# Attention loop of a two-block layer stack: query blocks from last to first, head outputs taken first, transposes ahead of the memory unit

## The chip, the cores and the metric

One core of one Trainium2 chip runs the whole program. The metric is the device time of one execution in microseconds. The times of before are those of 3 runs.

## What is computed

Two layers of a first block (gated short convolution, retention, squared-ReLU MLP) on 512 tokens of width 1024, and then one layer of a second block. The change lies in the second block's mixer, and in the rotary tables of the first. Cut to what matters:

```python
def nsa_mixer(q, k_c_raw, v_c_raw, k_s, v_s, k_w, v_w, gate_logits, ...):
    ...
    s_c = einsum(qb, k_cmp) * scale            # 31 compressed keys
    p_c = masked_softmax(s_c, cmp_end <= t)
    ...                                        # 8 key blocks, 16 to be chosen: all are
    p_s = masked_softmax(s_s, kpos <= t)
    p_w = masked_softmax(s_w, (kp <= t) & (kp > t - WINDOW))
    ...
    o = g0 * o_c + g1 * o_s + g2 * o_w

def gmlp_mixer(z, ...):                        # v normalised, mixed over 128 tokens
    return u * mixed
def conformer_conv_mixer(z, ...):              # 31 taps, layer norm, silu
    ...
def memory_cross_attention(x, mem, ...):       # k, v from 256 memory tokens
    ...
def rotary(t, positions):                      # first block: cos and sin of the angles
    ...
```

With 512 tokens the selected and the window attention are both plain causal attention, for 8 heads of width 64 in 2 key groups.

## The kernel before, in words

Everything is kept transposed: features on partitions, 512 tokens in the free dimension. Each matrix product is cut in units of 128 output columns. For a unit SyncE loads 512 KB of weights into one of two `raw` buffers, ScalarE rounds them to fp32r (`wh`, L451 in straight code, L504 in the layer loop), GpSimd subtracts to get the rest (`wl`, L422, two halves), and TensorE does 24 matmuls, high by high, high by low and low by high, in one of two PSUM banks. A load waits for the `wl` of two units before, ScalarE's split for the matmuls of four units before.

**The start.** ScalarE splits x and the first four weight units, then waits for the rotary angles from VectorE (L484), takes sine and cosine (L485, L486) and enters its loop over the two layers (L493). There `ahead(VV, f)` waits for unit f's matmuls and splits unit f + 4, and after f = 3 the square root of the mean square is taken (L491). The eight units VV are of another form (L1708): four token blocks in four banks, and the second four of them use `aux`; its bank 3 also holds the mean square, so that TensorE waits for the root before it starts on that bank.

**The attention loop.** After the input products of the second block come 16 steps. `ITS` lists pairs (c, rp), query block c of 128 tokens and head pair rp, and each pair has two steps b = 0, 1 (selected and window attention), each with 4 heads. Step k has scores against (c + 1) * 128 keys. A list `TURNS` gives the blocks of 128 probabilities to be transposed: for b = 0 the compressed block (31 keys) and c + 1 others, for b = 1 c + 1. In each iteration k of the written-out loops:

- TensorE (L1969): the ones-matmul of a norm at steps 3, 7, 8 and 10 (`mixer_norms`, L1884), the scores of step k + 1 (L1897, after the exps of step k), one unit of the memory's keys or values (`mem_unit`, L1780, 24 matmuls of 256 columns), then `values(k - 1)`: it waits for the weighed probabilities of step k - 1 and, for b = 0, for `o_taken`; it transposes block by block (L1917, L1919), and after each transpose multiplies the block before with the values (L1933), all into one bank, `unit_ps[1]`.
- ScalarE (L719): exps of heads 0 and 1 of step k + 1 (L669), copy of the memory unit (L714), split of the next weights (L451), then by turns the copy of a transposed block of step k - 1 (`take_turn`, L678) and exps of heads 2 and 3.
- VectorE (L1444): `shift(k + 1)` adds the mask on the diagonal block and takes the negative maximum (L1326, L1328), `weigh(k)` multiplies the four heads by gate over sum (L1336, L1342), for b = 1 `take_out(it - 1)` copies the finished outputs of the pair before (L1181), three taps of the 31-tap convolution (L1215; 62 in all, 36 of them before the loop), and pieces of the three norms (L1390, L1401, L1411, L1421, L1430). What is left of the taps is done at once before the sum of step 6.

Ahead of the loop stand the mixing over tokens (`mix_mm`, L1959, after the last query unit), its use on VectorE (L1382), and the compressed scores (L1903), which use the same two banks. Behind it, the squares of the attention outputs are summed and averaged (L1997), and the eight parts are normalised (L1471, L1478) for the first output unit (L1794), in the order of `PART_ORDER`.

## Time and profile before

| | us |
|---|---|
| median of 3 runs | 2635.04 |
| lowest, highest | 2633.44, 2638.72 |
| the profiled execution, own time | 2637.93 |
| its span | 2636.1 |
| TensorE busy (with overlaps of pipelined matmuls taken out) | 2542.3 (96%) |
| VectorE busy | 1237.7 (47%) |
| ScalarE busy | 907.2 (34%) |
| GpSimd busy | 1252.6 (48%) |
| granted TensorE clock, mean | 0.979 |

A granted clock of 1.00 is 2.4 GHz, 0.50 is 1.2 GHz. Spans of back-to-back matmuls overlap in the trace: the distance of their starts is what one costs.

### The profile page before, as it was taken

To read this page: it belongs to the slowest core of one execution; us is meant where nothing else is said; L and a number is where in the kernel's file an instruction comes from. 1 tells how busy PE (TensorE), PEld (TensorE's weight loads), DVE (VectorE), ACT (ScalarE), POOL (GpSimd) and SP (SyncE) were. 2 spreads that over 40 slices of the span, in tenths; PEclk is the share of its full clock that TensorE was granted. 3 is DMA by queue.
4 is the path that set the end of the run, shared out by engine and by line. 5 is a ranking of instruction groups with operands and counts; after the bars stand their busy time and mean duration, and the time that the engine had idled before them with its cause. 6 is when DMAs were issued, how large, how long until landed. Compare 5 with 4: busy or idle time off the path is not lost.

```text
span 2636.1 us, 34492 instructions
## 1 busy us (share of the span) xinstructions
PE 2542.3 (96%) x11696; PEld 2056.3 (78%) x11696; DVE 1237.7 (47%) x1471; ACT 907.2 (34%) x1281; POOL 1252.6 (48%) x879
## 2 busy tenths in 40 slices
PE   8999999999999999999999999999777799999998
PEld 6887788888888888877888888888644487888887
DVE  5434612452322543451245332268776654788373
ACT  4223433332222422343333222243345433444233
POOL 4554355555555555534555554555322142555454
PEclk8999999999999999999999999999888899999999
DMA  4333133333333333323333333363111031333332
GB/s 146 100 95 88 56 96 96 97 95 98 99 96 98 93 101 96 92 59 88 96 96 96 96 96 97 102 152 89 57 48 41 25 95 48 96 96 96 98 99 74
DMA packets 448120, 236.23 MB, mean 90 GB/s; under 512 B 16144, under 2 KB 442256, under 8 KB 447888
## 3 DMA queue, kind: packets, MB, share of 16 engines
q1 hardware_dynamic: 446896, 232.38, 30.6%
q10 hardware_dynamic: 1120, 2.51, 0.3%
q8 instruction: 61, 1.00, 0.2%
q14 instruction: 43, 0.35, 0.0%
HBM read 232.76 MB, written 2.10 MB: 89 GB/s over the span
## 4 chain that ended last, share of the span: by engine, by line
PE 89%; DVE 6%; issue 2%; ACT 1%; POOL 1%; DMA 0%; DVEq 0%; ACTq 0%; POOLq 0%
PE unit_ps L1673 58%; PE unit_ps L1794 16%; PE unit_ps L1780 7%; PE aux L1708 2%; PE o_banks L1738 1%; DVE a_f L1342 1%; DVE row L1328 1%; PE unit_ps L1933 1%; DVE c_f L1215 1%; PE aux L1726 1%; POOL wl L422 1%; PE o_banks L1919 1%; PE aux L2009 1%; DVE aux L1326 0%; PE unit_ps L1708 0%
## 5 line engine op out<-in xcount | busy, mean ns | idle before, releaser
L422 POOL TENSOR_TENSOR wl<-raw,wh 128x512 fp32r<-128x512 f32 x862 | 1246.1, 1466 | 1363.4 <-ACT wh L504 853.3
L504 ACT ACTIVATE wh<-raw 128x1024 fp32r<-128x1024 f32 x304 | 322.3, 1061 | 1028.1 <-PE unit_ps L1673 975.3
L1673 PE MATMUL unit_ps<-ah,wh 128*128 128x512 f32 x1280 | 503.5, 393 | 3.6 <-DVE tmp L1072 3.6
L1673 PE MATMUL unit_ps<-al,wh 128*128 128x512 f32 x1280 | 499.5, 390 | 0.0
L1673 PE MATMUL unit_ps<-ah,wl 128*128 128x512 f32 x1280 | 499.5, 390 | 0.0
L1673 PE MATMUL unit_ps<-bh,wh 128*128 128x512 f32 x768 | 299.7, 390 | 0.0
L1673 PE MATMUL unit_ps<-bl,wh 128*128 128x512 f32 x768 | 298.8, 389 | 0.0
L1673 PE MATMUL unit_ps<-bh,wl 128*128 128x512 f32 x768 | 298.8, 389 | 0.0
L1673 PEld LDWEIGHTS unit_ps<-ah,wh 128*128 128x128 f32 x1280 | 241.2, 188 | 55.9 <-DVE tmp L1072 4.4
L1673 PEld LDWEIGHTS unit_ps<-al,wh 128*128 128x128 f32 x1280 | 240.9, 188 | 51.4 <-issue 1.9
L1673 PEld LDWEIGHTS unit_ps<-ah,wl 128*128 128x128 f32 x1280 | 241.1, 188 | 50.5
L451 ACT ACTIVATE wh<-raw 128x1024 fp32r<-128x1024 f32 x111 | 117.6, 1060 | 205.3 <-PE unit_ps L1794 111.9
L1673 PEld LDWEIGHTS unit_ps<-bh,wh 128*128 128x128 f32 x768 | 144.2, 188 | 30.8 <-issue 1.0
L1673 PEld LDWEIGHTS unit_ps<-bl,wh 128*128 128x128 f32 x768 | 144.2, 188 | 30.3 <-issue 0.5
L1673 PEld LDWEIGHTS unit_ps<-bh,wl 128*128 128x128 f32 x768 | 144.2, 188 | 29.9
L1146 DVE TENSOR_TENSOR x<-unit_ps,x 128x512 f32 x48 | 33.2, 691 | 213.5 <-PE unit_ps L1673 213.5
L1794 PE MATMUL unit_ps<-ch,wh 128*128 128x512 f32 x320 | 124.5, 389 | 0.0
L1794 PE MATMUL unit_ps<-cl,wh 128*128 128x512 f32 x320 | 124.5, 389 | 0.0
L1794 PE MATMUL unit_ps<-ch,wl 128*128 128x512 f32 x320 | 124.5, 389 | 0.0
L1136 DVE TENSOR_TENSOR tmp<-unit_ps,rstd 128x512 f32<-128x512 f32 x64 | 44.2, 691 | 135.7 <-PE unit_ps L1673 134.9
L1569 DVE SCALAR_TENSOR_TENSOR d<-tmp,vectors,d 128x511 f32<-128x511 f32 x88 | 106.1, 1205 | 1.5
L1673 PE MATMUL unit_ps<-ch,wh 128*128 128x512 f32 x256 | 99.6, 389 | 0.0
(349 smaller groups left out, 3876.6 us busy)
## 6 DMA issues: line engine op xcount, KB each, us to landing
raw<-w_in_dram SPq DMA_DIRECT2D x147, 512.0 KB, 4.0
raw<-w_up_dram SPq DMA_DIRECT2D x64, 512.0 KB, 4.0
raw<-w_down_dram SPq DMA_DIRECT2D x64, 512.0 KB, 4.0
raw<-up_dram SPq DMA_DIRECT2D x44, 512.0 KB, 3.8
raw<-w_conv_out_dram SPq DMA_DIRECT2D x16, 512.0 KB, 4.0
raw<-w_ret_out_dram SPq DMA_DIRECT2D x16, 512.0 KB, 3.9
raw<-w_o_dram SPq DMA_DIRECT2D x16, 512.0 KB, 4.0
raw<-down_dram SPq DMA_DIRECT2D x16, 512.0 KB, 3.8
```

Of the source, the lines that this page charges most:

```text
L422: last = pool.tensor_tensor(wl[j][:, half], raw[j % 2][:, half], wh[j][:, half].bitcast(F32), ALU.subtract)
L451: act.activation(wh[j][:], raw[j % 2][:], ACT.Copy).then_inc(w_hi, 1)
L504: act.activation(wh[j][:], raw[j % 2][:], ACT.Copy).then_inc(w_hi, 1)
L1136: dve.tensor_tensor(tmp[0][:], unit_ps[j % 2][:], rstd[:], ALU.mult).then_inc(evac, 1)
L1146: dve.tensor_tensor(blk(x, f), unit_ps[j % 2][:], blk(x, f), ALU.add).then_inc(evac, 1)
L1215: did(dve.scalar_tensor_tensor(out=cv_a[i], in0=src, scalar=w, in1=cv_a[i], op0=ALU.mult, op1=ALU.add))
L1328: did(dve.tensor_reduce(row[:, 4 * b, heads], aux[:, heads, 0:nk], AX, ALU.max, negate=True), shift_att)
L1569: did(dve.scalar_tensor_tensor(out=into, in0=tmp[n % 2][:, 0:T - s_], scalar=ffn_taps[:, w_, b:b + 1], in1=into, op0=ALU.mult, op1=ALU.add ...
L1673: last = pe.matmul(unit_ps[j % 2][:], w[j][:, k], v[:, k * T:(k + 1) * T], start=(k == 0 and n == 0), stop=(k == KB - 1 and n == 2))
L1708: last = pe.matmul(v_ps[group][c], v[:, col:col + P], two_k(w[j])[:, k], start=(k0 + k == 0 and w is wh and v is ah), stop=(k0 + k == KB - ...
L1780: last = pe.matmul(dst, w[u % 4][:, k], v[:, k * n:(k + 1) * n], start=(k == 0 and q == 0), stop=(k == n_k - 1 and q == 2))
L1794: last = pe.matmul(unit_ps[u % 2][:], w[u % 4][:, k], v[:, k * T:(k + 1) * T], start=(at == 0 and q == 0), stop=(at == n_k - 1 and q == 2))
```

## The change

It does seven things. The query blocks go from c = 3 to c = 0 (`ITS`). VectorE does `take_out` before `shift` and `weigh`. TensorE transposes the first two blocks of step k - 1 before the memory unit, and the others two ahead of the values; ScalarE copies them before exps 0 and 1 of step k + 1. The convolution's sums and norm move from step 7 to step 9, with three taps in every step until then. The mixing over tokens goes ahead of the last query unit, and its VectorE part too, in the place of two taps. The reciprocal for the norm of x goes to step 7, its products from steps 13 and 14 to steps 14 and 15. At the start, sine and cosine go behind the square root of the first layer, and ScalarE's loop over the two layers is written out.

```diff
-ITS = [(c, rp) for c in range(NC) for rp in range(REP // 2)]
+ITS = [(c, rp) for c in reversed(range(NC)) for rp in range(REP // 2)]
...
-GM_STEP, CV_STEP = 3, 7
+GM_STEP, CV_STEP, TAPS_IN_STEP = 3, 9, 3
...
# ScalarE
-            act.wait_ge(ang_done, 1)
-            act.activation(sin[:], sin[:], ACT.Sin).then_inc(trig_done, 1)
-            act.activation(cos[:], cos[:], ACT.Sin).then_inc(trig_done, 1)
-            act.wait_ge(ones_set, 1)
...
-            with act.Fori(0, LAYERS) as l:
+            for l in range(LAYERS):
...
                     if f == 3:
                         sqrt_ms(l * 2 + 1)
+                        if l == 0:
+                            act.wait_ge(ang_done, 1)
+                            act.activation(sin[:], sin[:], ACT.Sin).then_inc(trig_done, 1)
+                            act.activation(cos[:], cos[:], ACT.Sin).then_inc(trig_done, 1)
...
-                if more:
-                    exp_head(k + 1, 0)
-                    exp_head(k + 1, 1)
+                turns = turns_of(k - 1)
+                for n in range(2):
+                    if n < len(turns):
+                        take_turn(*turns[n])
+                    if more:
+                        exp_head(k + 1, n)
                 mem_copy(k)
                 ahead2(MK + k)
-                turns = turns_of(k - 1)
-                for n in range(max(len(turns), 2)):
-                    if n < len(turns):
-                        take_turn(*turns[n])
-                    if more and n < 2:
-                        exp_head(k + 1, 2 + n)
+                for turn in turns[2:3]:
+                    take_turn(*turn)
+                if more:
+                    exp_head(k + 1, 2)
+                for turn in turns[3:4]:
+                    take_turn(*turn)
+                if more:
+                    exp_head(k + 1, 3)
+                for turn in turns[4:]:
+                    take_turn(*turn)
...
# VectorE
             z_query(2)
-            some_taps(2)
+            dve.wait_ge(mix_mm, 2)
+            for i in range(2):
+                ...
+                mult(y_gm[i], gm_u[i], tmp[1][:], mixed)
             z_query(3)
...
-                elif k == CV_STEP + 5:
+                elif k == CV_STEP - 2:
                     go()
                     did(dve.reciprocal(rstd_x, rstd_x))
-                if k in (CV_STEP + 6, CV_STEP + 7):
+                if k in (CV_STEP + 5, CV_STEP + 6):
                     for n in range(4):
-                        first_norm(4 * (k - CV_STEP - 6) + n)
+                        first_norm(4 * (k - CV_STEP - 5) + n)
...
                 mixer_norms_first(k)
+                if b == 1 and it:
+                    take_out(it - 1)
                 if k + 1 < N_STEPS:
                     shift(k + 1, 0)
                     shift(k + 1, 1)
                 if k == 0:
                     compressed_weights()
                 weigh(k)
-                if b == 1 and it:
-                    take_out(it - 1)
-                some_taps(3)
+                some_taps(TAPS_IN_STEP)
                 mixer_norms_last(k)
...
# TensorE
-            for f in range(Z_KW, Z_Q + 4):
+            for f in range(Z_KW, Z_Q + 3):
                 z(f)
...
+            def first_turns(k):
+                it, b, c, rp = STEPS2[k]
+                if b == 0:
+                    pe.wait_ge(pc_ready, 1)
+                pe.wait_ge(p_ready, k + 1)
+                for j in turns_of(k)[:2]:
+                    turn_block(j)
+
             def values(k):
                 it, b, c, rp = STEPS2[k]
-                mine = [j for j, turn in enumerate(TURNS) if turn[0] == k]
-                pe.wait_ge(p_ready, k + 1)
-                if b == 0:
-                    pe.wait_ge(pc_ready, 1)
-                    if it:
-                        pe.wait_ge(o_taken, it)
+                if b == 0 and it:
+                    pe.wait_ge(o_taken, it)
+                mine = turns_of(k)
                 for j in mine:
-                    turn_block(j)
-                    if j > mine[0]:
-                        block_values(j - 1)
-                block_values(mine[-1])
+                    block_values(j)
+                    if j + 2 <= mine[-1]:
+                        turn_block(j + 2)
...
                         if i and c == NC - 1:
                             last.then_inc(mix_mm, 1)
+            z(Z_Q + 3)
...
-                mem_unit(k)
                 if k == 0:
                     pe.wait_ge(shift_cmp, 1)
                 else:
+                    first_turns(k - 1)
+                mem_unit(k)
+                if k:
                     values(k - 1)
+            first_turns(N_STEPS - 1)
             values(N_STEPS - 1)
```

## Rows read from the trace of the kernel before

**Rows 1.** Stretches: length; busy PE, PEld, DVE, ACT, POOL; clock; DMA share, GB/s.
```profile
100.00:1750.00 1650.00, 1646.25 (x7185) 1346.58 (x7184) 614.64 (x751) 510.63 (x615) 837.30 (x581) 1.00 0.33 95
1866.30:2096.40 230.10, 167.06 (x1028) 113.26 (x1027) 160.41 (x245) 105.48 (x239) 45.35 (x34) 0.82 0.14 42
```

**Rows 2.** Waits of TensorE, 1866 to 2097 us: total, times, longest.
```profile
PE o_banks L1917 <- DVE d L1181: 22.2, 7, 5.6
PE unit_ps L1933 <- ACT a_f L678: 10.4, 14, 1.6
```

**Rows 3.** Waits of VectorE, the same stretch.
```profile
DVE aux L1326 <- PE aux L1897: 35.5, 8, 9.8
...
DVE d L1401 <- PE unit_ps L1884: 2.2, 1, 2.2
```

**Rows 4.** ScalarE in order of time, at the start: start, length, what, wait before it.
```profile
21.07 1.28 ACT L485 ACT_TABLE_LOAD   x1
34.50 0.63 ACT L485 ACTIVATE sin_t<-sin_t 128x512 f32<-128x512 f32 x1 [12.15 <-DVEq L895]
...
36.96 2.00 ACT L504 ACTIVATE wh<-raw 128x1024 fp32r<-128x1024 f32 x2
...
49.07 0.69 ACT L491 ACTIVATE rstd<-aux,eps 128x512 f32<-128x512 f32 x1
```

**Rows 5.** TensorE in order of time, at the start.
```profile
38.07 1.22 PE L1708 MATMUL aux<-wh,ah 128*128 128x512 f32 x2 [5.20 <-ACT wh L504]
...
49.81 1.22 PE L1708 MATMUL aux<-wh,ah 128*128 128x512 f32 x2 [3.16 <-ACT rstd L491]
...
69.05 0.39 PE L1673 MATMUL unit_ps<-ah,wh 128*128 128x512 f32 x1
```

**Rows 6.** SyncE's queue: the issue of the load of unit 4.
```profile
21.70 0.37 SPq L321 DMA_DIRECT2D raw<-w_in_dram  x1
```

**Rows 7.** The same load, then that of unit 6: KB, us to landing.
```profile
raw<-w_in_dram SPq DMA_DIRECT2D x1, 512.0 KB, 5.3
...
raw<-w_in_dram SPq DMA_DIRECT2D x1, 512.0 KB, 3.6
```

**Rows 8.** GpSimd in order of time, low parts of units 4 and 5.
```profile
38.10 4.97 POOL L422 TENSOR_TENSOR wl<-raw,wh 128x512 fp32r<-128x512 f32 x4 [13.02 <-ACT wh L504]
```

**Rows 9.** TensorE in order of time, ahead of the loop.
```profile
1866.24 1.97 PE L1959 MATMUL o_banks<-d,c_f 128*64 128x128 f32 x32
...
1872.02 6.88 PE L1903 MATMUL o_banks<-k_cmp,c_f 64*128 64x31 f32 x64 [3.17 <-DVE d L1177]
```

**Rows 10.** VectorE in order of time, in the loop and behind it.
```profile
1891.38 1.25 DVE L1342 TENSOR_SCALAR a_f<-a_f,row 128x128 f32<-128x128 f32 x4
...
1895.56 0.42 DVE L1328 TENSOR_REDUCE row<-aux 128x2 f32<-128x256 f32 x1
...
1897.49 3.20 DVE L1342 TENSOR_SCALAR a_f<-a_f,row 128x128 f32<-128x128 f32 x4
...
2010.09 1.23 DVE L1328 TENSOR_REDUCE row<-aux 128x2 f32<-128x1024 f32 x1
...
2067.54 2.05 DVE L1342 TENSOR_SCALAR a_f<-a_f,row 128x512 f32<-128x512 f32 x4
...
2081.66 0.43 DVE L1181 COPY d<-unit_ps 128x256 f32<-128x256 f32 x1 [11.54 <-PE unit_ps L1933]
```

**Rows 11.** TensorE in order of time, in the loop: at half clock, then at full.
```profile
2022.12 1.12 PE L1919 MATMUL o_banks<-ident,a_f 128*128 128x128 f32 x4
...
2025.07 2.34 PE L1897 MATMUL aux<-c_f 64*128 64x512 f32 x8
...
2030.32 0.82 PE L1919 MATMUL o_banks<-ident,a_f 128*128 128x128 f32 x6
...
2072.81 0.65 PE L1933 MATMUL unit_ps<-a_f,c_f 128*64 128x256 f32 x4
2073.40 0.66 PE L1919 MATMUL o_banks<-ident,a_f 128*128 128x128 f32 x4
```

More of the change, by code:

```diff
@@ L1314, in _ @@
             z_query(2)
-            some_taps(2)
+            dve.wait_ge(mix_mm, 2)
+            for i in range(2):
+                go()
+                biased = tmp[1][:].rearrange("p (c t) -> p c t", c=NC)
+                did(dve.tensor_tensor(biased, o_ps[i].rearrange("p (c t) -> p c t", c=NC), gm_bias[:, i].unsqueeze(1).broadcast_to([P, NC, P]), ALU.add))
+                mult(y_gm[i], gm_u[i], tmp[1][:], mixed)
             z_query(3)
@@ L1376, in compressed_weights @@
                 mult(p_cmp, p_cmp, by_head.unsqueeze(3).broadcast_to([P, 2, NC * REP, N_CMP]), pc_ready)
-            dve.wait_ge(mix_mm, 2)
-            for i in range(2):
-                go()
-                biased = tmp[1][:].rearrange("p (c t) -> p c t", c=NC)
-                did(dve.tensor_tensor(biased, o_ps[i].rearrange("p (c t) -> p c t", c=NC), gm_bias[:, i].unsqueeze(1).broadcast_to([P, NC, P]), ALU.add))
-                mult(y_gm[i], gm_u[i], tmp[1][:], mixed)
             shift(0, 0)
@@ L1935, in block_values, with turns_of @@
                         last.then_inc(o_att, 1)
+            def turns_of(k):
+                return [j for j, turn in enumerate(TURNS) if turn[0] == k]
+            def first_turns(k):
[5 more added lines that the diff above has]
+                    turn_block(j)
             def values(k):
                 it, b, c, rp = STEPS2[k]
-                mine = [j for j, turn in enumerate(TURNS) if turn[0] == k]
-                pe.wait_ge(p_ready, k + 1)
-                if b == 0:
-                    pe.wait_ge(pc_ready, 1)
-                    if it:
-                        pe.wait_ge(o_taken, it)
+                if b == 0 and it:
+                    pe.wait_ge(o_taken, it)
+                mine = turns_of(k)
                 for j in mine:
-                    turn_block(j)
-                    if j > mine[0]:
-                        block_values(j - 1)
-                block_values(mine[-1])
+                    block_values(j)
+                    if j + 2 <= mine[-1]:
+                        turn_block(j + 2)
             pe.wait_ge(gm_ready, 1)
```

## The prediction

> **What bounds the kernel now.** I read the stages first. From 100 to 1750 us TensorE is busy for 1646 of 1650 us at full clock [rows 1]: nothing on ScalarE, VectorE or GpSimd can help or hurt there as long as it stays hidden. The first 100 us and the attention stretch (1866 to 2096 us, TensorE busy 167 of 230 us, granted clock 0.82) are where an order of instructions can matter. Then I read the waits of that stretch. TensorE waits 22.2 us before the first transpose of a query block (L1917), seven times for the VectorE copy at L1181, which is `take_out` [rows 2]. VectorE waits 35.5 us for score matmuls [rows 3] and 11.5 us for the last values [rows 10]. So the two wait for each other in turn; the loop is a chain, and neither is full. The reader is to see that `take_out(it-1)` needs values finished long ago, but stands behind `shift(k+1)` and `weigh(k)`.
>
> **Part 1, the sine and cosine.** ScalarE loads the Sin table at 21.07, stands until 34.50 for VectorE's angles, reloads, and only at 36.96 splits weight unit 4 [rows 4]. Behind it hang the unit's low part, the next two loads, the square root at 49.07, and TensorE: it starts unit 4 at 38.07, stops before bank 3 and goes on at 49.81 with 78 matmuls left until 69.05 [rows 5]. After the change the split waits for the data alone. The load was issued at 21.70 [rows 6] and took 5.3 us [rows 7]: 27.0. Then split 1.05 (28.1), low part 2.5 (30.6; four halves took 4.97 [rows 8]), low part of unit 5 another 2.5 (33.1), load of unit 7 3.6 [rows 7] (36.7), its split 1.05, table load 1.28, root 0.69: 39.8 against 49.8. **Minus 10.0 us.** TensorE is free for unit 4 at 32.9 (38.07 less its wait of 5.20 [rows 5]); 18 matmuls of 0.229 (1646 us for 7185 [rows 1]) bring it to bank 3 at 37.0, so it stands 2.8 us, where before it stood twice. Before, the last 78 matmuls took 19.2 us instead of 17.8, the first of them at half clock; if the clock stays at 2.4 GHz another 1.4 us go. Bounds: minus 7 (loads later behind the decay table) to minus 11.5. Sin and cos themselves (1.2 us and a table load) now follow the root, beside matmuls, and end near 42; VectorE, in its 3.35 us reciprocal, asks for them later. If that cover went they would cost 2.5 us. Unrolling the layer loop on ScalarE touches only the stretch where TensorE is full: 0, bounds plus or minus 1 (one more or less table load of 1.28 a layer).
>
> **Part 2, the memory mixing ahead of the last query unit.** Now z(Z_Q+3) ends, mixing takes 1.97, and TensorE waits 3.17 us for VectorE before the compressed scores at 1872.02, which then take 6.88 us with 64 matmuls [rows 9], at 1.2 GHz. After: query unit 3 ends 2 us later (1868.3), one evacuation of about 0.7, scores of step 0 for four key blocks 2.0 (2.3 in rows 11, partly at half clock): 1871, with no wait. At full clock the 64 take about half, ending at 1875; at half clock at 1878. I take 1875. But steps 0 and 1 are now blocks of 512 keys: VectorE's reduction is 1.23 instead of 0.42 [rows 10], two per shift, so shift(1) costs 1.6 more, weigh(0) 0.8 more (2.05 against 1.25, rows 10). `weigh(0)` ended at 1892.63. **Minus 1.5**, bounds plus 1.5 to minus 3. The two taps left out here come back in the loop.
>
> **Part 3, the loop.** From the end of weigh(0), 1892.63, to the end of the last copy before the drain, 2070.1 (2081.66 less the wait of 11.54 [rows 10]), VectorE spends 177.5 us; 35.5 + 2.2 are waits [rows 3], so 139.8 is work. After: two of the long shifts and one weigh moved out in front, minus 3.3 and 0.8; two taps more, plus 1.6. Then collisions: a weigh of four 128x128 took 3.20 us while GpSimd subtracted a weight unit and 1.25 us while it didn't [rows 10], 1.95 per unit. Of the 16 units I count six whose subtraction now falls in VectorE's waits or reciprocals; with the waits gone about three more collide, plus 5.5. Work 142.8.
> Waits: `take_out` first costs VectorE 0.5 us in another place and nothing new, since TensorE finished those values one iteration before. It frees TensorE's 22.2 us. Transposes of two blocks ahead of the memory unit hide ScalarE's copies behind 24 matmuls (the waits for them at L1933 were 10.4 us [rows 2]). TensorE's own period for four key blocks is per pair of steps 2 x 2.0 scores, 2 x 3.0 memory units (from the scores' end to 2030.32), 9 blocks of 1.2 (transposes and values, 0.66 and 0.65 long, each beginning a little before the other ends) = 20.8 [rows 11]; VectorE's is about 21. For one key block 11.5 against 14 with reciprocals. So VectorE bounds, and its waits go except in the convolution's norm chain: there TensorE's mean waits for VectorE's sum and VectorE for the mean. These now lie in steps 9 to 12. From each step's durations I get 2 us at step 9 (the mean), 5.5 at step 10 (the variance behind a memory unit at half clock) and 3.5 in steps 11 to 13: 11 in all, bounds 4 and 24 (the waits at the chain now). Sum 153.8 against 177.5: **minus 23.7**. The five taps in a lump before step 7 go into steps 7 and 8, the same work. The reciprocal of rstd_x at step 7 and first_norm one step later are moved, at 0.
>
> **Part 4, the drain.** VectorE is through at 2070.1, and the next copy waits 11.54 us until 2081.66 [rows 10], because the last two steps have five and four blocks to transpose and multiply. With blocks from last to first it is two and one, and VectorE still has four norm products to do: 0.5 remains. **Minus 11.0**, bounds minus 8 and 11.5. The 14.3 us from there to TensorE's restart don't change.
>
> **ScalarE and the queues.** exp_head now stands behind take_turn, so behind `weigh(k-1)`; that one ended before the shift whose result exp_head needs, so 0. If weigh ran late each exp would slip with it. Weight loads are issued per unit as before, one in 6 us or more.
>
> **Sum.** 10.0 + 1.5 + 23.7 + 11.0 = 46.2 off the profiled execution's 2637.9: 2591.7. The median of the runs is 2.9 lower than that execution, so I give 2589.
>
> **A rule against it.** In the rows a collision costs 1.95 us per unit, and the rest of the two subtractions runs beside VectorE. The Trainium skill, "SBUF — State Buffer", section "Who interferes with whom", says the pair of ports that VectorE and GpSimd share is an exclusive lock and the loser fully blocks for the whole instruction. By that rule every unit could cost its whole subtraction.
>
> **Rivals.**
> A. *Collisions fill the gain.* If all 16 units blocked VectorE for their 2.5 us, that is 40 us against the about 17 lost now, plus 23 instead of plus 5.5: 2606. For it: VectorE is now dense. Against: rows 10 show 1.95, and reciprocals and shifts run free. 0.12.
> B. *The norm chain stays single file.* All 24 us of waits stay in the short last steps, where TensorE has least to do: 2602. For it: the longest wait, 9.8 [rows 3], was there. 0.14.
> C. *The start doesn't shrink*, since loads of units 6 and 7 come later: 2599. 0.05.
> D. *The other side: TensorE stays at 1.2 GHz through the loop.* At full clock it has 48 blocks x 1.2 + 16 x 3.0 + 24 of scores = 130 us; at half a transpose group lasts 1.12 instead of 0.66 [rows 11], 1.7 times as long: 221 us against today's 199 from 1882.9 to 2081.66, plus 22, less 4 for the earlier start and 10 of part 1: 2643. It decides once TensorE spends some four fifths of the loop at half clock. The clock is 0.82 today, and the half-clock pieces follow the waits for take_out, which go. 0.04.
> E. *The order was not the limit*: something I don't see holds the pair, and only part 1 offsets new frictions: within 0.2% of before. 0.02.
> The forecast itself, 2577 to 2598: 0.57; still lower, 0.06.
>
> **The numbers.** Low 2574 is all parts at their good bounds nearly (11.5 + 3 + 35 + 11.5); high 2612 takes in A, B and C and A with B in part. A measurement of this kernel tells 0.2% (5 us) from no change. Faster 0.94, same 0.02, slower 0.04.
>
> **What would show it.** In the changed profile: the root before unit 4's bank 3 near 40 and the first L1673 matmul near 58; no wait of L1917 for L1181; VectorE's score waits about 11 us, at steps 9 to 12; the last take_out within 2 us of the norm products; output units going on near 2050 of the new span, where they did at 2096. Wrong if TensorE's clock in the loop is under 0.6, or if VectorE's taps and weighs average more than a third above today's.

## The result, and the profile after

| | before | after |
|---|---|---|
| median, us (4 runs each) | 2634.24 | 2590.52 |
| lowest, highest | 2632.62, 2638.72 | 2589.98, 2591.71 |
| the profiled execution, own time | 2637.93 | 2590.40 |
| its span | 2636.1 | 2588.6 |
| TensorE busy | 2542.3 (96%) | 2524.0 (98%) |
| granted TensorE clock, mean | 0.979 | 0.986 |

The ratio of the runs is 0.9835 (95% interval 0.9822 to 0.9847): the changed kernel is 43.7 us faster by the medians. The profiled executions are 47.5 us apart, because that of before lies 3.7 us above its own median. Sums over stages below are of those two executions.

The changed kernel by stretches: length; busy PE, PEld, DVE, ACT, POOL; clock; DMA share, GB/s. The rows are the step ahead of the loop, the loop to the last copy, the drain to TensorE's restart, and all that is behind it.

```profile
1859.60:1881.80 22.20, 14.67 (x112) 8.82 (x112) 18.87 (x27) 11.22 (x23) 5.17 (x4) 0.80 0.17 48
1881.80:2034.10 152.30, 129.25 (x872) 90.50 (x872) 129.72 (x203) 86.70 (x205) 40.12 (x30) 0.91 0.17 49
2034.10:2048.90 14.80, 6.80 (x11) 2.99 (x11) 12.39 (x15) 7.21 (x11) 0.00 (x0) 0.59 0.12 33
2048.90:2588.60 539.70, 527.08 (x2361) 431.54 (x2361) 322.53 (x317) 211.14 (x295) 260.82 (x184) 0.99 0.29 86
```

The reader is to compare the second row with the kernel before over the same work:

```profile
1892.60:2070.10 177.50, 130.11 (x760) 85.76 (x760) 129.39 (x201) 84.51 (x196) 37.90 (x29) 0.83 0.14 42
```

VectorE is busy for about the same 129 us (its gaps between instructions not counted) in 152 us instead of 177. The work did not shrink; the standing did. Where the 47.5 us between the spans came from:

| stretch | before | after | difference | predicted |
|---|---|---|---|---|
| start, to the first 512-column unit | 69.05 | 61.59 | −7.5 | −10.0 |
| from there to the end of `weigh(0)` | 1823.6 | 1820.2 | −3.4 | −1.5 |
| loop, to the end of VectorE's last work before the last copy | 177.5 | 152.2 | −25.3 | −23.7 |
| that end to the start of the last copy | 11.5 | 0.1 | −11.4 | −11.0 |
| start of the last copy to the end | 554.4 | 554.5 | 0 | 0 |

Waits of TensorE in the changed kernel, 1856 to 2052 us (total, times, longest), against [rows 2]:

```profile
PE unit_ps L1938 <- ACT a_f L677: 9.2, 12, 2.5
...
PE unit_ps L1889 <- DVE d L1395: 4.6, 1, 4.6
...
PE o_banks L1922 <- DVE d L1187: 1.4, 1, 1.4
```

L1187 is `take_out`, L1922 and L1924 are the transposes (L1917 and L1919 before), L1938 the values. The 22.2 us for `take_out` are 1.4 now. The waits for ScalarE's copies of the key blocks are still there, 9.2 for 10.4: the copies stand ahead of the memory unit only for the first two blocks.

Waits of VectorE there, against [rows 3]:

```profile
DVE aux L1337 <- PE aux L1902: 10.8, 3, 5.7
DVE d L1406 <- PE unit_ps L1889: 2.2, 1, 2.2
```

One of the three, 1.26 us, is before `weigh(0)` ends. In the loop itself 9.6 + 2.2 = 11.8 us are left of 37.7.

VectorE in order of time (start, length, what, wait before it), against [rows 10]: a weigh and three taps beside GpSimd, the norm's mean, the score waits of steps 10 and 12, and the last copy.

```profile
1888.29 2.95 DVE L1353 TENSOR_SCALAR a_f<-a_f,row 128x512 f32<-128x512 f32 x4
1891.27 3.21 DVE L1221 SCALAR_TENSOR_TENSOR c_f<-hp,vectors,c_f 128x512 f32<-128x512 f32 x3
...
1971.27 1.41 DVE L1406 TENSOR_TENSOR d<-c_f,unit_ps 128x512 f32<-128x512 f32 x2 [2.17 <-PE unit_ps L1889]
...
1982.41 0.43 DVE L1337 TENSOR_TENSOR aux<-aux,diag 128x256 f32<-128x256 f32 x1 [3.84 <-PE aux L1902]
...
2003.17 0.43 DVE L1337 TENSOR_TENSOR aux<-aux,diag 128x256 f32<-128x256 f32 x1 [5.72 <-PE aux L1902]
...
2034.14 0.42 DVE L1187 COPY d<-unit_ps 128x256 f32<-128x256 f32 x1
```

The last copy waited 11.54 us before and follows at once now.

The start, ScalarE in order of time, against [rows 4]:

```profile
27.63 1.06 ACT L499 ACTIVATE wh<-raw 128x1024 fp32r<-128x1024 f32 x1 [6.18 <-DMA raw<-w_in_dram]
...
38.04 1.06 ACT L499 ACTIVATE wh<-raw 128x1024 fp32r<-128x1024 f32 x1 [1.88 <-DMA raw<-w_in_dram]
39.11 1.28 ACT L486 ACT_TABLE_LOAD   x1
40.41 0.69 ACT L486 ACTIVATE rstd<-aux,eps 128x512 f32<-128x512 f32 x1
```

and TensorE there, against [rows 5]:

```profile
36.74 0.61 PE L1713 MATMUL aux<-wl,ah 128*128 128x512 f32 x2
41.15 1.22 PE L1713 MATMUL aux<-wh,ah 128*128 128x512 f32 x2 [3.80 <-ACT rstd L486]
42.17 1.05 PE L1713 MATMUL aux<-wh,al 128*128 128x512 f32 x2
...
47.05 0.63 PE L1713 MATMUL aux<-wh,al 128*128 128x512 f32 x2
...
61.59 0.39 PE L1678 MATMUL unit_ps<-ah,wh 128*128 128x512 f32 x1
```

The root ends at 41.10 instead of 49.76. But TensorE stood 3.80 us for it and comes back at half clock: a pair of matmuls has 1.05 us until 46.4 and 0.62 after.

### The profile page after: what moved, and what is told of

It reads as the page before. It is cut to its first block, busy times and chain, and to the rows that moved or that the text cites. A ratio compares the mean times of both kernels' runs of the same rounds, so it can differ in the third digit from the quotient of the medians.

```text
span 2588.6 us, 34392 instructions
## 1 busy us (share of the span) xinstructions
PE 2524.0 (98%) x11696; PEld 2044.5 (79%) x11696; DVE 1243.3 (48%) x1471; ACT 904.0 (35%) x1278; POOL 1255.5 (48%) x879
## 4 chain that ended last, share of the span: by engine, by line
PE 89%; DVE 7%; issue 1%; ACT 1%; POOL 1%; DMA 0%; DVEq 0%; POOLq 0%; ACTq 0%
PE unit_ps L1678 59%; PE unit_ps L1799 16%; PE unit_ps L1785 7%; PE aux L1713 2%; PE o_banks L1743 1%; DVE a_f L1353 1%; DVE c_f L1221 1%; DVE row L1339 1%; PE aux L1731 1%; POOL wl L422 1%; PE aux L2026 1%; PE unit_ps L1713 0%; PE unit_ps L2086 0%; DVE aux L1337 0%; PE aux L2044 0%
```

## The experiments

Twelve kernels, each timed against the kernel before on the same chip (medians of before 2634.0, 2633.5 and 2634.1 in the three groups that ran together). The last column sets their medians beside that of the change, 2590.52, which was timed in a group of its own. The first four have one part of the change alone, the next five the whole change but one part, one has two parts together, and two try to go further. All but the last only rearrange work that the two kernels have.

| kernel | median | ratio, 95% interval | against before | against the change |
|---|---|---|---|---|
| start alone | 2624.86 | 0.9965 (0.9955 to 0.9976) | −9.2 | |
| take_out first alone | 2615.67 | 0.9932 (0.9915 to 0.9949) | −18.3 | |
| transposes ahead alone | 2618.42 | 0.9943 (0.9927 to 0.9960) | −15.6 | |
| blocks reversed alone | 2623.13 | 0.9963 (0.9950 to 0.9975) | −10.9 | |
| without take_out first | 2594.81 | 0.9852 (0.9835 to 0.9868) | | +4.3 |
| without the reversal | 2594.88 | 0.9855 (0.9838 to 0.9871) | | +4.4 |
| without transposes ahead | 2596.90 | 0.9859 (0.9842 to 0.9875) | | +6.4 |
| convolution norm back | 2589.65 | 0.9829 (0.9813 to 0.9845) | | −0.9 |
| mixing back | 2592.14 | 0.9833 (0.9815 to 0.9852) | | +1.6 |
| take_out and transposes | 2609.99 | 0.9904 (0.9887 to 0.9920) | −24.1 | |
| root ahead of unit 7 | 2589.04 | 0.9823 (0.9807 to 0.9840) | | −1.5 |
| the same, TensorE kept busy | 2589.29 | 0.9822 (0.9806 to 0.9839) | | −1.2 |

The intervals of the three rows with +4.3 to +6.4 still overlap that of the change (0.9822 to 0.9847). But every run of these three kernels (lowest 2592.24) is slower than every run of the change (highest 2591.71). So that they lose something is shown; how much is known only to some 2 or 3 us.

### Start alone

```diff
-            act.activation(sin[:], sin[:], ACT.Sin).then_inc(trig_done, 1)
-            act.activation(cos[:], cos[:], ACT.Sin).then_inc(trig_done, 1)
...
-            with act.Fori(0, LAYERS) as l:
+            for l in range(LAYERS):
...
+                        if l == 0:
+                            act.wait_ge(ang_done, 1)
+                            act.activation(sin[:], sin[:], ACT.Sin).then_inc(trig_done, 1)
+                            act.activation(cos[:], cos[:], ACT.Sin).then_inc(trig_done, 1)
```

> The kernel before with the start alone: sine and cosine behind the square root, ScalarE's layer loop written out. Theory: the first unit with L1673-type matmuls starts 7.5 us earlier, as in the changed kernel (61.6 us against 69.05), and nothing else moves: minus 7.5 us, 2627. Rival (the written-out loop does something of its own in the 1650 us of layers): differs from minus 7.5 by more than 1.5 us, with the difference between 100 and 1740 us.

Measured 9.2 us by the medians. That is 1.7 more than the 7.5 expected, and by its size on the rival's side of the line. But the difference isn't where the rival puts it: from the first 512-column unit to the end of `weigh(0)` this trace has 1822.9 us, that of before 1823.6. The first 512-column unit is at 61.45 instead of 69.05, so 7.6 are the start's own in this pair of traces. Over all traces it is more: that unit starts at 69.05 to 70.66 in the five kernels with the old start (mean 70.0) and at 59.97 to 61.59 in the seven with the new one (mean 60.5), 9.5 us apart, which agrees with the 9.2 of the medians. The attention loop, whose code is that of before, took 184.3 us from the end of `weigh(0)` to the last copy, where the profiled execution of before had 189.0. Two rows over that loop, the kernel before and then this one:

```profile
1892.60:2081.60 189.00, 140.63 (x833) 91.39 (x834) 129.41 (x201) 89.64 (x205) 40.35 (x30) 0.84 0.14 43
```

```profile
1884.30:2068.60 184.30, 139.01 (x834) 90.08 (x834) 128.31 (x201) 89.83 (x205) 41.16 (x30) 0.86 0.15 44
```

The same instructions, a slightly higher clock, and 32.0 us of score waits for 35.5. So two profiled loops of the same code can differ by 5 us. The prediction rested on one that is among the longer (its execution is 3.7 above the median), and a stage's difference of a few us between two profiles is not to be read as the effect of an edit.

### take_out first alone

```diff
+                if b == 1 and it:
+                    take_out(it - 1)
                 if k + 1 < N_STEPS:
                     shift(k + 1, 0)
...
-                if b == 1 and it:
-                    take_out(it - 1)
```

> The kernel before with take_out ahead of shift and weigh alone. Theory (the order of VectorE is what TensorE waited for): the seven waits of the first transpose for L1181, 22.2 us, go, and most of VectorE's waits for scores with them, since its scores hang behind those values; 15 to 20 us off in all, 2615 to 2620, and the granted clock of the loop rises from 0.83 to about 0.9. Rival (the transposes ahead of the memory unit are the main part; without them the wait moves to weigh): under 8 us off, and TensorE waits at the first transpose for L1342 instead.

18.3 us, within the expected range. The two waits of the pair, TensorE's and then VectorE's, same stretch as [rows 2, 3]:

```profile
PE unit_ps L1933 <- ACT tmp L678: 16.9, 8, 4.8
```

```profile
DVE aux L1326 <- PE aux L1897: 11.3, 4, 8.6
DVE d L1181 <- PE unit_ps L1933: 8.9, 1, 8.9
```

The 22.2 us at L1917 for `take_out` are gone, and another wait has grown in their place: 16.9 us, eight times, for ScalarE's copy of the first transposed block (`tmp`, the compressed one), where the kernel before had 5.8. One step of two hung there on two things, and freeing one bares the other. VectorE's score waits fall from 35.5 to 11.3 all the same, and the granted clock of the loop to the last copy rises from 0.84 to 0.92. The wait of the last copy falls too, from 11.5 to 8.9, though the order of the blocks is that of before.

### Transposes ahead alone

```diff
+                    first_turns(k - 1)
+                mem_unit(k)
+                if k:
                     values(k - 1)
```

with `first_turns`, the two-block lead in `values` and ScalarE's order as in the change.

> The kernel before with the first two transposes ahead of the memory unit and ScalarE's order to match, alone. Theory: the first value matmuls still wait for take_out, which still stands behind shift and weigh; only two transposes and two copies per step come out of the chain: 5 to 8 us off, 2626 to 2629. Rival (this is the main part): 15 us or more.

Measured 15.6 us, about twice the expectation and near its rival. What TensorE waits for at `take_out` in it:

```profile
PE unit_ps L1940 <- DVE d L1188: 15.9, 6, 5.0
...
PE o_banks L1924 <- DVE d L1188: 4.4, 1, 4.4
```

The waits put down to `take_out` shifted mostly from the first transpose (L1917, 22.2) to the first multiplication with the values (L1940). Together they are 20.3, hardly less than before; what has changed is that the transposes and their copies are done ahead of them. Score waits fell from 35.5 to 18.7. I had taken this part as worth only the 10.4 us of waits for copies; it is worth also what it hides of the other one.

### Blocks reversed alone

```diff
-ITS = [(c, rp) for c in range(NC) for rp in range(REP // 2)]
+ITS = [(c, rp) for c in reversed(range(NC)) for rp in range(REP // 2)]
```

> The kernel before with query blocks from last to first, alone. Theory: the drain (VectorE's wait of 11.5 us at the last take_out) shrinks by 8 to 10 us, the start of the loop costs 2.4 us (two long shifts and a weigh in front), the loop itself stays a chain: 6 to 8 us off, 2626 to 2628. Rival (total work between the two engines is the same, so what the drain gives the start takes): within 2 us of before.

Measured 10.9, more than expected, and by another way. The copies of its drain:

```profile
2057.44 0.42 DVE L1181 COPY d<-unit_ps 128x256 f32<-128x256 f32 x1
2065.03 0.42 DVE L1181 COPY d<-unit_ps 128x256 f32<-128x256 f32 x1 [7.17 <-PE unit_ps L1933]
```

The wait of the last copy falls only from 11.54 to 7.17. The rest is in the loop, where score waits are 28.7 for 35.5: the convolution's norm chain (steps 8 to 10) now falls into steps of two key blocks rather than three, and the long steps come while VectorE still has taps to do. Which of the two counts is argued here, not shown.

### Without take_out first

```diff
-                if b == 1 and it:
-                    take_out(it - 1)
                 if k + 1 < N_STEPS:
...
                 weigh(k)
+                if b == 1 and it:
+                    take_out(it - 1)
```

> The changed kernel with take_out back behind weigh. Theory: it loses 10 to 18 us of the 43.7: TensorE waits at the first value matmul for L1187, once per pair of steps, ratio to the kernel before 0.988 to 0.991. Rival (with the transposes ahead the wait is hidden): loses under 4 us.

Only 4.3 us are lost, where the part alone gave 18.3; less than expected and nearer the rival. The wait did return, at the values:

```profile
PE unit_ps L1938 <- DVE d L1187: 12.4, 6, 3.6
```

12.4 us of TensorE's waits, but VectorE's score waits went from 10.8 to 16.5 us only, and the loop is 3.9 us longer (156.1 for 152.2). TensorE has slack in this loop (129 busy of 152 us), so most of the 12.4 is taken out of idle time that it had anyway. This is the reading that carries the rest: once the transposes are ahead, `take_out` in its old place is late for TensorE but seldom for VectorE, and VectorE sets the pace.

### Without the reversal

```diff
-ITS = [(c, rp) for c in reversed(range(NC)) for rp in range(REP // 2)]
+ITS = [(c, rp) for c in range(NC) for rp in range(REP // 2)]
```

> The changed kernel with query blocks from first to last again. Theory: the drain comes back (last take_out waits about 8 to 10 us instead of 0), the long blocks lie with the norm chain, which then costs less wait; loses 6 to 10 us in all, ratio 0.986 to 0.988. Rival: loses 2 us or less, since waits of the norm chain (13 us now) go when long steps lie beside it.

4.4 lost, less than expected. `weigh(0)` ends 1.5 us earlier after the first 512-column unit (small blocks come first, but the stretch varies by more than that between kernels), the loop to the last copy is 158.8 for 152.3, and the last copy waits 2.77 us, not 11.5. So nearly 9 of the 11.5 us of the drain's wait go without the order of the blocks.

### Without transposes ahead

```diff
-                    first_turns(k - 1)
                 mem_unit(k)
...
+                    turn_block(j)
+                    if j > mine[0]:
+                        block_values(j - 1)
```

> The changed kernel with TensorE's and ScalarE's old order of transposes. Theory: VectorE bounds the loop (13 us of waits in 152), so TensorE's longer period for four and three key blocks shows only in part: loses 4 to 8 us, ratio 0.985 to 0.987. Rival (the transposes ahead are the main part): loses 12 us or more, and VectorE's waits for scores grow by as much.

6.4 lost, the most of the three by the medians, and within what was expected. VectorE's waits for scores grow from 10.8 to 16.4, as much as without take_out first. The wait for ScalarE's copy of the compressed block, 1.8 us in the changed kernel, is back:

```profile
PE unit_ps L1931 <- ACT tmp L677: 15.2, 8, 5.6
```

### Convolution norm back to steps 7 to 10

```diff
-GM_STEP, CV_STEP, TAPS_IN_STEP = 3, 9, 3
+GM_STEP, CV_STEP, TAPS_IN_STEP = 3, 7, 3
...
-                elif k == CV_STEP - 2:
+                elif k == CV_STEP + 5:
...
-                if k in (CV_STEP + 5, CV_STEP + 6):
+                if k in (CV_STEP + 6, CV_STEP + 7):
```

> The changed kernel with the convolution's norm back at steps 7 to 10 (seven taps in a lump at step 6, first products at 13 and 14). Theory: the same VectorE work, the waits of the norm chain (13 us) now lie beside blocks of three and two keys where TensorE has more to do: within 3 us of the changed kernel, either way. Rival (the later steps were the point of this part): slower by 5 us or more, waits at steps 7 to 10 over 18 us.

No difference that can be told (0.9829 against 0.9835, intervals over each other). TensorE's mean waits 10.1 us for VectorE's lump of taps, VectorE's score waits are 11.8 us for 10.8, and the last copy waits 3.27: the norm products end a step earlier and no longer cover it. What the move cost in one place it gave back in the other.

### Mixing back behind the last query unit

```diff
-            for f in range(Z_KW, Z_Q + 3):
+            for f in range(Z_KW, Z_Q + 4):
...
-            z(Z_Q + 3)
```

with VectorE's use of it behind the compressed scores again.

> The changed kernel with the mixing back behind the last query unit and its two taps back. Theory: the compressed scores wait again 3 us for VectorE and run at half clock (6.9 instead of 3.7 us): step 0's weigh ends 3 to 4 us later, two taps of 0.8 to 1.1 us leave the loop: slower than the changed kernel by 1 to 3 us. Rival: same within 1 us, since VectorE's chain there does not hang on them.

1.6 us slower by the medians, as expected, with intervals that overlap, so the size isn't settled. In the trace TensorE waits 1.9 us before the compressed scores and takes 6.61 us for them, at half clock, where the change has 3.66. Their result is used 1809.4 us after the first 512-column unit instead of 1804.3; the loop is 1.9 us shorter in return.

### take_out first and transposes ahead together

The two diffs above, in the kernel before.

> The kernel before with take_out first and the transposes ahead, together and alone. Theory (the two remove the same waits, since both take TensorE's values out of the chain through VectorE): 22 to 27 us off, not the 34 that they give one by one (18.3 and 15.6): 2607 to 2612. Rival (they add up): 32 us or more off.

24.1 us, as expected, where the two alone have 18.3 + 15.6 = 33.9. Some ten of them are the same ten: both parts end waits of one chain. Its last copy waits

```profile
DVE d L1188 <- PE unit_ps L1940: 5.7, 1, 5.7
```

with blocks still from first to last.

### Root ahead of unit 7

A try at the remaining 3.80 us of the start: the first layer's root stands ahead of ScalarE's split for unit 7, behind which it hung.

```diff
                 for f in range(KB):
-                    ahead(VV, f, f % 4)
                     if f == 3:
                         sqrt_ms(l * 2 + 1)
+                    ahead(VV, f, f % 4)
+                    if f == 3:
                         if l == 0:
```

> The changed kernel with the first layer's square root ahead of the split of weight unit 7 instead of behind it. Theory (the root hangs behind the load of unit 7, which landed 1.3 us later than I had worked out): the root ends near 35 us, TensorE goes through bank 3 without its wait of 3.8 us and without the half-clock matmuls behind it, and the first unit with 512-column matmuls starts near 56.5 instead of 61.6: 4 to 5 us off the changed kernel. Rival (the low part of unit 5 or the load of unit 6 is as late): under 1.5 us off, with a wait for the weights in its place.

1.5 us less by the medians, not 4 to 5: the size that the rival gave (under 1.5), and not told apart from the change by the intervals. Its ScalarE and TensorE at the start:

```profile
37.02 1.06 ACT L499 ACTIVATE wh<-raw 128x1024 fp32r<-128x1024 f32 x1 [5.82 <-DMA raw<-w_in_dram]
...
39.40 0.69 ACT L486 ACTIVATE rstd<-aux,eps 128x512 f32<-128x512 f32 x1
```

```profile
40.13 0.74 PE L1714 MATMUL aux<-wh,ah 128*128 128x512 f32 x2 [1.57 <-ACT rstd L486]
```

The root now hangs behind the load of unit 6, which in this execution landed some 2 us later than in the changed kernel (split at 37.02, there 35.09). TensorE waits 1.57 us and keeps its full clock: a pair has 0.74, not 1.22, and the 78 matmuls to the first 512-column unit at 57.99 take 17.9 us, not 20.4. That unit comes 3.6 us earlier than in the change. But the stretch behind it was 2.0 us longer (1822.3 for 1820.2), and 1.48 of these are a wait that no kernel with a later start has: two units on, at 70.51, TensorE stands for VectorE's rotary products (L978). The next kernel has the same start, and in its trace unit 6 came 2.4 us sooner: root at 36.96, 0.64 us of waiting, the first 512-column unit at 55.52, 6.1 us ahead of the change. There TensorE stands 2.94 us for the same products, until 69.50, and runs at half clock soon after. An earlier root doesn't pay beyond a few us, since another chain is next. VectorE's reciprocal begins at 44.16 (44.31 in the change), whatever the root does. ScalarE takes the values of the tokens from 49.89 on, and behind them in its order stand the next splits, at 53.49 and 62.14, then the second half of the values, and VectorE's rotary products last.

### The same, with TensorE kept busy in the drain

Eight matmuls (sixteen in the trace) whose result nobody reads, four before the mean of the attention norm and four inside the first output unit, to hold the clock through the drain (0.59 granted in the changed kernel's).

```diff
+            def keep_busy(n):
+                for _ in range(n):
+                    pe.matmul(unit_ps[0][:], mean_d[:], mem_vt[:, 0:T], start=True, stop=True)
+            keep_busy(4)
...
+                        if at == 3:
+                            keep_busy(4)
```

> b_root, and eight more matmuls in the drain, whose results nobody reads: four before the mean of the attention squares and four while the first output unit waits for its fourth block. Theory (TensorE falls to 1.2 GHz in the drain, and its mean matmul of 2.07 us, nine matmuls and some of the next fifteen run at half clock): the mean takes 1.1 us, the unit goes on at full clock, 2 to 3 us off b_root. Rival (the clock isn't held by them, or they end after the data are there): within 1 us of b_root or slower.

Nothing gained. TensorE in the drain:

```profile
2040.30 1.02 PE L2020 MATMUL aux<-d,mean_n 128*128 128x512 f32 x2
...
2043.93 0.50 PE L2030 MATMUL unit_ps<-ah,wh 128*128 128x512 f32 x1 [0.61 <-DVE al L1484]
...
2049.19 0.50 PE L2030 MATMUL unit_ps<-ah,wh 128*128 128x512 f32 x1 [0.86 <-DVE al L1484]
```

The clock is full (the mean's two matmuls take 1.02 us, in the changed kernel 2.07). But the blocks of the first output unit wait 0.3 to 0.9 us each for VectorE's normalised block, and the unit goes on 14.8 us after the last copy, as in the change. The first four extra matmuls even end late, after the sum is there: the mean starts 5.9 us after the last copy instead of 4.0, and still nothing moves. The drain belongs to VectorE and ScalarE; TensorE's speed there was not on the path. By its size this is the rival that the expectation named, and one of its two reasons is true (they end after the data); the other isn't, since the clock was held.

## Why the prediction was right, and where it was not

2589 was predicted, 2590.5 is the median. Against the profiled execution of before the sum was 2591.7, and the changed kernel's profiled execution took 2590.4. The mechanism was right, two engines that wait for each other in turn until VectorE's work is the bound. That the number is so near is in part luck: in these two executions the terms are off by 2.5, 1.9, 1.6 and 0.4 us, with both signs, and two executions of the same stage differ by as much. The terms one by one:

**The start, −10.0 predicted, −7.5 measured.** The order of events was right, and in this pair of executions two terms were off. The root ended at 41.1, not 39.8: the load of unit 4 came 0.6 us later than the sum had it, and with that and the steps behind it the load of unit 7 1.3 us later (split at 38.04, predicted 36.7). In the six other kernels with this start the root ends at 40.6 to 40.8, so 0.8 to 1.3 late in all of them. And the sum kept 19.2 us for the 78 matmuls, with 17.8 as what a full clock would give: TensorE stood 3.80 us, not 2.8, came back at half clock, and they took 20.4. 1.3 + 1.2 are the 2.5 missing. The 1.2 are chance, not an effect of the longer stand: of the seven kernels with this start five took 19.3 to 19.5 us for the 78 matmuls, near the sum's 19.2, and the means over all kernels are 9.5 us apart, not 7.5. The sign that the prediction gave, the first 512-column unit near 58, counts another 1.4 us for a full clock that its sum left out; no kernel with the root behind unit 7 came under 59.97. That the 17.8 I had put is right for the full clock is shown by the kernel with the root ahead of unit 7 (17.9). Sine and cosine behind the root cost TensorE nothing here, but not for the reason given. VectorE asks for them ahead of its reciprocal, not behind it, and waits 0.89 us for them at 43.86. It is late itself: GpSimd's low parts now run from 28.78 to 34.36 and from 36.23 on, beside VectorE's work on the angles, which took 14.9 us (27.7 to 42.6) where it had taken 7.0 (27.4 to 34.4) with GpSimd idle. So the reciprocal begins at 44.31, 3.2 us after the root. The prediction has no term for this collision; it was hidden behind TensorE's matmuls, and it is what the kernels with the root moved ran into. The root's switch of table is one row of 1.28 us, 39.11 to 40.39, with the root at 40.41 and sine's load straight at 41.12. The Trainium skill, "ScalarE: Activation LUTs", section "What ACT_TABLE_LOAD costs", adds a drain of some 1.4 us to each switch, about 2.7 in all; no such gap is in these rows, on either side of the load. Had it been there, each root would have come later by as much.

**Mixing and compressed scores, −1.5 predicted, −3.4 measured.** The compressed scores behave as put: no wait, and 64 matmuls at full clock.

```profile
1862.20 3.66 PE L1908 MATMUL o_banks<-k_cmp,c_f 64*128 64x31 f32 x64
```

3.66 us for 6.88, and the wait of 3.17 gone [rows 9]. The 1.9 us more than predicted can't all be put to this edit. With the mixing taken out, the last query unit ends 1.3 us earlier after the first 512-column unit than before (1795.9 for 1797.2), and no edit touches TensorE up to there: this stretch differs by several us between kernels that have the same code in it (below).

**The loop, −23.7 predicted, −25.3 measured.** The 177.5 us of before are on the long side: the start-alone kernel, with the same loop, took 172.7 to the same point, and against that one the loop is 20.5 shorter. So this term holds to some 3 us and no better. Inside it are two errors of opposite sign. Waits: 11 predicted, 11.8 measured. 2.2 at step 9 as worked out; at step 10 3.84 instead of 5.5; and behind that 5.72, all at step 12, instead of 3.5. Part of the last has a cause that the prediction did not see, ScalarE. Its rows there:

```profile
1992.13 1.53 ACT L702 ACTIVATE d<-d,vectors 128x512 f32<-128x512 f32 x2 [1.67 <-DVE d L1183]
1993.57 1.14 ACT L705 ACTIVATE d<-d 128x512 f32<-128x512 f32 x2
1994.61 0.57 ACT L677 ACTIVATE tmp<-o_banks 31x512 f32<-31x512 f32 x1
```

and TensorE's:

```profile
1995.32 0.74 PE L1938 MATMUL unit_ps<-tmp,v_cmp 31*64 31x256 f32 x4 [1.75 <-ACT tmp L677]
...
1999.55 1.12 PE L1938 MATMUL unit_ps<-a_f,c_f 128*64 128x256 f32 x4 [0.94 <-ACT a_f L677]
2000.60 2.08 PE L1889 MATMUL unit_ps<-d,mean_v 128*128 128x512 f32 x2
2002.61 0.72 PE L1902 MATMUL aux<-c_f 64*128 64x128 f32 x8
```

ScalarE waits for VectorE's product, does the convolution's silu, and copies the compressed block only then; values, the norm's mean at half clock and the scores follow, and VectorE stands until 2003.17. "exp_head and the copies: 0" was right for the steps without a norm and not for this one.

Work: 142.8 predicted, 152.2 − 11.8 = 140.4 measured, 139.8 before. VectorE's groups in the loop of the changed kernel (busy, mean ns of one, idle before):

```profile
L1353 DVE TENSOR_SCALAR a_f<-a_f,row 128x384 f32<-128x384 f32 (+3 forms) x61 | 31.6, 517 | 2.2
L1221 DVE SCALAR_TENSOR_TENSOR c_f<-hp,vectors,c_f 128x512 f32<-128x512 f32 x28 | 28.3, 1010 | 1.0
L1339 DVE TENSOR_REDUCE row<-aux 128x2 f32<-128x768 f32 (+3 forms) x28 | 21.5, 767 | 1.0
...
L1199 DVE SCALAR_TENSOR_TENSOR x<-x,vectors,tmp 128x512 f32<-128x512 f32 x8 | 8.7, 1090 | 0.3
```

The same four had 34.1, 24.2 (26 of them), 24.7 and 6.9 us before (L1342, L1215, L1328, L1193).
The reductions lost 3.2 us (3.3 predicted). The other three groups changed by −2.5, +4.1 and +1.8, together +3.4; of that a short weigh in the place of a long one (−0.8) and two taps more (+1.6) are 0.8, and the 2.6 left are more collisions with GpSimd, for 5.5 predicted. The price per collision was about right, the count too high. It was too high for the kernel before too: by the durations of the same instructions with GpSimd idle, an estimate, the three groups lost 13.8 us before, where the prediction had about 17, and lose 16.4 now. In the rows of VectorE above, one GpSimd unit (1889.40 to 1892.36) stretched four weighs from 2.05 to 2.95 us and three taps from 2.33 to 3.21: 1.8 us per unit, and GpSimd's own two halves took 2.96 instead of 2.49. By the rule of the exclusive lock that the prediction quotes from the Trainium skill ("SBUF — State Buffer", section "Who interferes with whom"), the whole subtraction would be lost each time. These rows disagree with it in size: VectorE loses 0.9 of each half of 1.25 us, some seven tenths, and all of it together takes 6.2 us where one after the other would be 6.9. Rival A is out: it had the work at 23 us more than the reordered 137.3, so 160, where 140.4 were measured.

**The drain, −11.0 predicted, −11.4 measured, for a reason that was only partly right.** The prediction put it to the order of the blocks. The experiments distribute the 11.5 us of the wait otherwise: reversal alone leaves 7.17, take_out first alone 8.90, transposes alone all of the 11.54, take_out and transposes together 5.70, all but the reversal 2.77, all but the moved norm 3.27. No part alone makes it vanish, and none of these is needed for most of it. The last copy waits for the values of the last two steps, so all that lets TensorE arrive earlier and all that keeps VectorE busy until then (the four norm products in step 15 instead of step 14) shortens it.

**The parts do not add.** Alone they give 9.2 + 18.3 + 15.6 + 10.9 = 54 us, together, and with the two parts that were not tried alone, 43.7; taken back one at a time three of them cost 4.3 to 6.4, and the moved norm nothing. The sum of the prediction came out because it was not made edit by edit for the loop, but as VectorE's work plus the waits that stay. The three orders end largely the same waits, and once two are in, VectorE's work is the bound and the third has little left to take.

**The other rivals.** B (the norm chain keeps its 24 us) would have left some 24 of score waits; 11.8 are there. C is true only in its cause: the load of unit 7 was late, by 1.3 us, and the start shrank all the same. D: the clock in the loop rose from 0.83 to 0.91. E is out.

What stays open: how the gain of the reversal alone (10.9) divides between the place of the norm chain and the longer early steps; no run separates the two. And what makes most of the variation of the stretch in the middle (below).

## What to carry to other kernels

Where two engines wait for each other in turn, cost the loop as the fuller engine's work plus the waits that no reordering can reach, not as a sum of gains by edit: here three edits worth 18, 16 and 11 us alone were worth 4 to 6 each once the others were in. Before an engine is made faster or kept at its clock, read who waits for whom in that very stretch: TensorE at full clock in the drain gained nothing, since every block there waited for VectorE. A profiled execution that lies above its median, as that of before does by 3.7 us, hides that much in its stages; compare its own time with the runs, and the stage with the same stage of other kernels, before its few us are explained. And an engine that is moved earlier meets other neighbours: here the earlier low parts on GpSimd doubled the time of VectorE's angles.

## What the runs showed of the hardware

- In the changed kernel TensorE stood 3.80 us behind the root and came back at half clock (1.05 us a pair until 46.4 us); its 78 matmuls took 20.4 us. The length of the stand alone doesn't say it: without the reversal it stood 3.59 us, came back at full clock, fell to half some 1 us later, and took 19.4; with the convolution's norm back it stood only 2.02 us, fell 1.5 us after it came back, and took 19.5. In the two kernels with the root moved it stood 1.57 and 0.64 us, stayed at full clock, and took 17.9 and 17.8.
- VectorE's angle work at the start took 7.0 us with GpSimd idle and 14.9 us beside 10.9 us of GpSimd's subtractions: 0.7 us lost for each of GpSimd's, as in the loop.
- The weight loads at the start, issued alike, were split at 27.63, 28.86 and 26.94 us in three kernels with the same code up to there, and the first 512-column unit of the changed kernel and of those with its start unchanged lies between 59.97 and 61.59.
- The stretch from that unit to the end of `weigh(0)`, whose code is nearly all the same, took 1818.7 to 1827.0 us over the fourteen kernels, and in the last two, which have the same code in all of it, 1822.3 and 1827.0. Of these two 1.48 and 2.94 us are the wait for the rotary products, and the second has some half-clock matmuls behind it. What makes up the rest, and the variation of the others, was not found; it is as large as some of the parts studied here, and differences under some 3 us in one trace mean nothing by themselves.
